# Input stage of a two-layer hybrid attention trunk: token norms from row sums through a diagonal product, norms in quarters, first weights loaded between the blocks of x

## The chip, the cores and the metric

One core of one Trainium2 chip runs the whole program. The metric is the device time in microseconds (us) of one execution; lower is better. Five engines work beside each other and meet only at semaphores: TensorE (PE), VectorE (DVE), ScalarE (ACT), GpSimd (POOL) and SyncE (SP), which here only issues transfers.

## The reference

1040 tokens (16 meta tokens, then 1024 of x) of width 1024 pass two layers. All is float32.

```python
def hybrid_layer(h, pos, norm_g, w_in, w_out, sinks):
    u = rmsnorm(h, norm_g)                       # u = h * rsqrt(mean(h*h) + 1e-6) * g
    proj = jnp.einsum('bld,de->ble', u, w_in)    # 1024 -> 3328
    sb_q, sb_k, sb_v, sb_g, sw_q, sw_k, sw_v, sw_g = jnp.split(proj, splits, axis=-1)
    sb_o = stick_breaking_attention(sb_q, sb_k, sb_v) * jax.nn.silu(sb_g)    # 8 heads of 64
    sw_o = sliding_window_gqa(rope(sw_q), rope(sw_k), sw_v, sinks) * jax.nn.silu(sw_g)
    return h + jnp.einsum('ble,ed->bld', concatenate([sb_o, sw_o]), w_out)

h = concatenate([meta, x])
for l in range(2): h = hybrid_layer(h, ...)
return rmsnorm(h, final_norm_g)[:, 16:]
```

## The kernel before

**Data.** Activations lie transposed: `X[:, k, :]` holds width rows 128k to 128k+127 of all 1040 tokens. Tokens are cut into three chunks, c0 of 400, c1 of 384 and c2 of 256 columns. A projection ("proj j c") is one 128-wide weight tile j times one chunk, for all 8 k. To keep float32 precision each operand is split in a high and a low part (`UH`, `UL` of the normed activations, `WH`, `WL` of the weights), and each k takes three matmuls: UH·WH, UL·WH (L728) and UH·WL (L733); 24 matmuls for a projection. The low part is a subtraction of two tensors in SBUF. The first four tiles of a layer are v, g, q and k of head pair 0 (j = 0, 1, 2, 3).

**Order.** `layer_steps` writes one list of steps, `STEPS`, for both layers. Every engine walks it and does its own part of each step, so the list is each engine's program order. A step that waits holds back all that stands behind it on that engine. Two PSUM banks take turns for the projections: a projection waits until the one two before it has been read. `v` is read by ACT (`vT` copy), `g` by an ACT sigmoid and a DVE product.

**Norm of a chunk.** Squares of X (ACT), sum over k (DVE), a product with `ones` that sums over partitions and gives every partition the row of sums (PE, L676), reciprocal root (ACT, L933), three DVE refinements over the chunk (L1188, L1191, L1194), eight DVE products `mix = X * par * y` (L1198), two ACT copies to `UH` (L939), and the low part `UL`: rows 0 to 3 by POOL (L1491), rows 4 to 7 by DVE (L1205).

**Start.** SP issues ident, meta, the eight blocks of x, then the weights j = 0 and 1. PE transposes each block (L690) into one of two banks; ACT and DVE copy halves to `X` (L948, L1218). In layer 0 the squares are taken over whole chunks of `X` (L959) and summed by a DVE reduction (L1211). When all blocks are in `X`, SP writes `X` to memory (`h_spill`, L627, eight transfers; the residual is read back later) and only then issues the weights j = 2 and on (L621). The split of j = 0 and 1 (`split_w`) comes behind all this: WH by DVE (L1246), WL by POOL (L1504); later weights have both on DVE (L1250). ACT issues the tables `stick`, `cosT`, `sinT` behind the last transposed block.

**Layer end.** The norm of c0 for the next layer is made between the last output projections, c1 and c2 at the next layer's start. After the last layer the same steps run, UH and UL of c0 included, though nobody reads these; then the normed tokens are transposed back and stored.

Of the kernel before, what the change touches and what calls it, by code (L numbers as in the profile page):

```python
# [21 lines left out]
F32 = mybir.dt.float32  # L22
# [13 lines left out]
EPS = 1e-6  # L36
# [55 lines left out]
WL_BY_DVE = range(2, 34)  # L92
# [20 lines left out]
def layer_steps():  # L113
# [5 lines left out]
    def sb_unit(p):  # L119
# [85 lines left out]
    steps = [("split_w", 0), ("split_w", 1)] + flat(sb_unit(0))  # L205
# [31 lines left out]
    for i, c in outs:  # L237
# [16 lines left out]
STEPS = layer_steps()  # L254


def ring_uses():
# [64 lines left out]
 PER_LAYER) = ring_uses()  # L322
LAST_BLOCK = [max(b for b in range(BLOCKS) if q_start(b) < a + width) for a, width in CHUNKS]
# [85 lines left out]
def build(nc, x, meta, params, w_in, w_out, ident_d, rope_d, stick_d, out, h_spill):  # L409
    with ExitStack() as ctx:  # L410
# [57 lines left out]
        wl_made = Tally(sem("wl_made"), TILES, 2)  # L468
        h_ready = Tally(sem("h_ready"), KT * 3, KT * 3)
# [118 lines left out]
        def squared_chunk(c):  # L588

            if c:  # L590
                return mix[:, :, chunk_uses(c)]
            return Vn[:, :, :].rearrange("p a d -> p (a d)")[:, 0:KT * CHUNKS[0][1]].rearrange("p (k n) -> p k n", k=KT)
# [19 lines left out]
        def _(sp):  # L612
            sp.dma_start(ident[:], ident_d).then_inc(ident_in, 16)
            for b in range(BLOCKS):
                sp.dma_start(staged_in(b), x[128 * (b - 1):128 * b, :] if b else meta).then_inc(x_in[b], 16)
            for l in range(DEPTH):
# [12 lines left out]
                for j in range(2):  # L629
                    load(j)  # L630
# [39 lines left out]
        def _(pe):  # L670
# [10 lines left out]
            for b in range(BLOCKS):  # L681
                pe.wait_ge(x_in[b], 16)
                nq = n_queries(b)
                for half in range(2):
                    use = 2 * b + half
                    if use >= 2:
                        pe.wait_ge(in_copied_a if use % 2 == 0 else in_copied_v, use // 2)
                    for i in range(4):
                        t = 4 * half + i
                        ins = pe.transpose(t_bank[use % 2][:, i * nq:(i + 1) * nq],  # L690
                                           staged_in(b)[:, 128 * t:128 * t + 128], ident[0:nq, 0:nq])
                    ins.then_inc(in_turned, 1)
# [4 lines left out]

            for l in range(DEPTH):
                def proj_slot(use):
# [4 lines left out]
                    else:  # L704
# [9 lines left out]
                def project(step):  # L714
# [11 lines left out]
                    for k in range(KT):  # L726
                        for u in (UH, UL):
                            pe.matmul(bank[:, 0:width], WH[:, j % 2, k, :], u[:, k, chunk_uses(c)],  # L728
                                      start=(k == 0 and u is UH), stop=False)
                        if k == 0 and c == 0 and j:  # L730
                            pe.wait_ge(wl_made.sem, wl_made.at(l, j + 1))
                        if c or j:
                            ins = pe.matmul(bank[:, 0:width], WL[:, j % 2, k, :], UH[:, k, chunk_uses(c)],  # L733
                                            start=False, stop=(k == KT - 1))
                    if c == j == 0:

# [809 lines left out]
```

## Time and profile before

| | us |
|---|---|
| median of 3 runs | 1322.46 (1320.25 to 1324.81) |
| the profiled execution, its own time | 1323.66 |
| its span in the trace | 1321.6 |
| PE busy | 1223.2 (93%) |
| PEld busy (weight loads, beside PE) | 1107.6 (84%) |
| DVE busy | 728.3 (55%) |
| ACT busy | 440.3 (33%) |
| POOL busy | 36.2 (3%) |

The span is what the hardware profiler saw from first to last instruction; 2.06 us of the execution's own time lie outside it. PE is busy in almost all of it, so what matters is where it is not, and at which clock it runs.

### The profile page before, as it was taken

How to read it: one execution, taken by the hardware profiler on the slowest of the kernel's cores; microseconds unless marked ns; L12 is line 12 of the kernel's file. 1: busy time of each engine (PE TensorE's matmuls, PEld its weight loads, DVE VectorE, ACT ScalarE, POOL GpSimd, SP SyncE). 2: the span in 40 equal slices, each digit the busy share in tenths (PEclk: the TensorE clock that was granted, in tenths of full speed). 3: DMA queues.
4: the chain of work that ended last, by engine and by line, in shares of the span. 5: the costliest groups of instructions: out<-in, count | busy, mean ns of one | idle time of the engine just before them, and what ended most of it. 6: DMA issues, size and time to landing. Idle time of an engine off the chain costs nothing.

```text
span 1321.6 us, 22286 instructions
## 1 busy us (share of the span) xinstructions
PE 1223.2 (93%) x8824; PEld 1107.6 (84%) x8824; DVE 728.3 (55%) x1376; ACT 440.3 (33%) x1169; POOL 36.2 (3%) x16
## 2 busy tenths in 40 slices
PE   4599999999999998899979999999999999889996
PEld 3598888888888887789969889888888888678995
DVE  5935546556466555734493554555546645573347
ACT  4313324333344342521131332333334333352113
POOL 1200000000000000000040000000000000000001
PEclk7699999999999997899979999999999989789997
DMA  4511101011012111042311101101101211104203
GB/s 163 201 49 32 28 22 33 19 31 33 18 39 62 30 43 39 15 148 65 129 64 49 33 18 32 33 17 33 33 18 39 59 33 39 43 6 157 65 0 127
DMA packets 101685, 69.29 MB, mean 52 GB/s; under 512 B 37824, under 2 KB 95168, under 8 KB 101584
## 3 DMA queue, kind: packets, MB, share of 16 engines
q1 hardware_dynamic: 100720, 66.55, 17.2%
q8 instruction: 71, 1.16, 0.4%
q10 hardware_dynamic: 864, 1.32, 0.3%
q14 instruction: 30, 0.25, 0.1%
HBM read 49.82 MB, written 12.71 MB: 47 GB/s over the span
## 4 chain that ended last, share of the span: by engine, by line
PE 82%; DVE 9%; ACT 4%; issue 3%; DMA 1%; SPq 0%; ACTq 0%; DVEq 0%
PE psum L728 38%; PE psum L733 18%; PE psum L781 7%; PE psum L810 6%; PE psum L793 6%; DVE mix L1198 2%; PE psum L842 2%; PE psum L872 1%; PE psum L879 1%; DMA w_raw<-in_w_out 1%; PE psum L854 1%; DVE dvT L1261 1%; PE psum L690 1%; DVE WH L1246 1%; DVE PT L1194 1%
## 5 line engine op out<-in xcount | busy, mean ns | idle before, releaser
L728 PE MATMUL psum<-UH,WH 128*128 128x384 f32 (+2 forms) x1632 | 551.5, 338 | 22.5 <-DVE WH L1246 10.4
L728 PE MATMUL psum<-UL,WH 128*128 128x384 f32 (+2 forms) x1632 | 535.4, 328 | 0.0
L733 PE MATMUL psum<-UH,WL 128*128 128x256 f32 (+2 forms) x1616 | 526.6, 326 | 0.9 <-DVE WL L1250 0.9
L728 PEld LDWEIGHTS psum<-UH,WH 128*128 128x128 f32 x1632 | 316.4, 194 | 36.8 <-DVE WH L1246 12.5
L728 PEld LDWEIGHTS psum<-UL,WH 128*128 128x128 f32 x1632 | 317.0, 194 | 0.5
L733 PEld LDWEIGHTS psum<-UH,WL 128*128 128x128 f32 x1616 | 312.0, 193 | 1.9 <-DVE WL L1250 1.8
L1093 ACT ACTIVATE PT<-psum 128x512 f32<-128x512 f32 (+5 forms) x260 | 116.7, 491 | 35.0 <-PE psum L793 18.3
L1084 ACT ACTIVATE X<-psum 128x264 f32<-128x264 f32 (+9 forms) x240 | 91.2, 432 | 77.1 <-PE psum L781 76.6
L1330 DVE TENSOR_TENSOR_SCAN X<-X,stick 16x16 f32<-16x16 f32 (+5 forms) x144 | 100.4, 737 | 24.8 <-ACT X L1084 24.4
L793 PE MATMUL psum<-ident,X 128*128 128x128 f32 x576 | 91.2, 283 | 3.7 <-ACT Vn L1047 2.7
L1333 DVE TENSOR_TENSOR_SCAN X<-X 128x352 f32<-128x352 f32 (+4 forms) x96 | 86.3, 939 | 7.5 <-ACT X L1084 7.5
L793 PEld LDWEIGHTS psum<-ident,X 128*128 128x128 f32 x576 | 61.9, 141 | 27.6 <-issue 23.1
L810 PE MATMUL psum<-PT,Vn 128*64 128x128 f32 (+1 forms) x1152 | 84.2, 281 | 0.0
L1250 DVE TENSOR_TENSOR WL<-w_raw,WH 128x1024 fp32r<-128x1024 f32 x64 | 78.4, 1225 | 2.2
L810 PEld LDWEIGHTS psum<-PT,Vn 128*64 128x64 f32 (+1 forms) x1152 | 61.0, 136 | 18.6 <-issue 18.2
L1246 DVE CAST WH<-w_raw 128x1024 fp32r<-128x1024 f32 x68 | 46.5, 686 | 38.4 <-issue 16.4
L975 ACT ACTIVATE mix<-X 128x400 f32<-128x400 f32 (+2 forms) x48 | 23.1, 492 | 133.7 <-DVE X L1269 131.5
L1360 DVE SCALAR_TENSOR_TENSOR mix<-psum,v_end,mix 128x128 f32<-128x128 f32 (+1 forms) x72 | 23.9, 332 | 78.6 <-PE psum L823 78.5
L1269 DVE TENSOR_TENSOR X<-psum,X 128x400 f32<-128x400 f32 (+2 forms) x48 | 24.6, 516 | 76.3 <-PE psum L733 76.3
L842 PE MATMUL psum<-SKH,SQ 64*128 64x144 f32 (+2 forms) x272 | 34.2, 309 | 28.6 <-ACT P_late L1107 15.5
L1491 POOL TENSOR_TENSOR UL<-mix,UH 128x1600 fp32r<-128x1600 f32 (+2 forms) x7 | 25.0, 3576 | 1240.1 <-DVE mix L1198 1228.6
L842 PEld LDWEIGHTS psum<-SKH,SQ 64*128 64x128 f32 (+1 forms) x272 | 26.6, 209 | 36.2 <-issue 29.6
(140 smaller groups left out, 1125.5 us busy)
## 6 DMA issues: line engine op xcount, KB each, us to landing
w_raw<-in_w_in SPq DMA_DIRECT2D x36, 512.0 KB, 3.8
h_spill<-X SPq DMA_DIRECT2D x16, 520.0 KB, 6.1
X<-h_spill SPq DMA_DIRECT2D x16, 520.0 KB, 5.7
w_raw<-in_w_in SPq DMA_DIRECT2D x32, 256.0 KB, 3.7
w_raw<-in_w_out SPq DMA_DIRECT2D x16, 256.0 KB, 3.1
w_raw<-in_w_out SPq DMA_DIRECT2D x32, 128.0 KB, 3.5
out<-X SPq DMA_DIRECT2D x6, 512.0 KB, 3.0
vT<-dvT SPq DMA_DIRECT2D x40, 50.0 KB, 2.0
```

Of the source, the lines that this page charges most:

```text
L728: pe.matmul(bank[:, 0:width], WH[:, j % 2, k, :], u[:, k, chunk_uses(c)], start=(k == 0 and u is UH), stop=False)
L733: ins = pe.matmul(bank[:, 0:width], WL[:, j % 2, k, :], UH[:, k, chunk_uses(c)], start=False, stop=(k == KT - 1))
L781: ins = pe.matmul(z_bank[0:n_queries(b), h, 0:hi - lo], QK[rows, q, queries], QK[rows, k, lo:hi], start=(i == 0), stop=(i == 2))
L793: ins = pe.transpose(bank[:, i * nq:(i + 1) * nq], weights(p, b, h)[:, a:a + 128], ident[:])
L810: ins = pe.matmul(o[64 * h:64 * h + 64, 0:nq], Vn[keys, 9 * (p % 2) + t, 64 * h:64 * h + 64], PT[keys, slots[h] % PT_RING, i * nq:(i + 1) ...
L842: ins = pe.matmul(z, q, keys[rows, first:first + count], start=(i == 0), stop=(i == 2))
L1084: act.activation(weights(p, b, h)[0:n_queries(b), lo:hi], z_bank[0:n_queries(b), h, 0:hi - lo], ACT.Sigmoid, scale=-SCALE).then_inc(z_read ...
L1093: act.activation(PT[0:rows, slot % PT_RING, 0:width], t_bank[use % T_RING][0:rows, 0:width], ACT.Copy)\
L1246: dve.tensor_copy(WH[:, j % 2, :, :], w_raw[:, j % 2, :, :]).then_inc(wh_made.sem, 1)
L1250: dve.tensor_tensor(WL[:, j % 2, :, :], w_raw[:, j % 2, :, :], WH[:, j % 2, :, :].bitcast(F32), ALU.subtract).then_inc(wl_made.sem, 1)
L1330: ins = dve.tensor_tensor_scan(down, down, edge, 1.0, ALU.mult, ALU.max)
L1333: ins = dve.tensor_tensor_scan(down, down, down, P[0:nq, hi:hi + 1], ALU.mult, ALU.bypass)
```

## The change

Layer 0 gets its own list (`LAYER_STEPS[0]`), which begins with the input blocks themselves. In it:

- ACT squares each block of x as it landed, tokens on partitions, and its accumulator gives the sum per token (`in_square`). The root and the three refinements are made on 4 (then 5) numbers a partition. DVE multiplies ident with them, which gives a diagonal matrix (`in_diagonals`), and PE's product of `ones` with it puts the factors in a row on all partitions, in PSUM (`in_rows`). The chunk reductions L1211 and squares L959 are gone.
- The transposed blocks use four banks, not two.
- SP issues w0 behind the second block of x and w1 behind the third. Only w0's low part is left to POOL, in layer 0.
- In both layers the products, UH and UL of a chunk are made in quarters (2 of 8 k), each quarter's UL by DVE; the first projection of a chunk starts when the first quarter is there. POOL does nothing after w0.
- The first projection does its three matmuls for each k like the others.
- Behind the last layer UH and UL of c0 are left out.
- ACT's copy of q, pair 0, now waits for the spill.

```diff
+def norm_pieces(c, ahead):
+    sc, hi, lo = ([(kind, c, part, ahead) for part in range(4)] for kind in ("scale", "high", "low"))
+    return sc[:2] + hi[:1] + lo[:1] + sc[2:3] + hi[1:2] + lo[1:2] + sc[3:] + hi[2:3] + lo[2:3] + hi[3:] + lo[3:]
+IN_GROUPS = [(0, 4), (4, 9)]
+def start_steps(proj_of):
+    T, S, C = ([(kind, b) for b in range(BLOCKS)] for kind in ("in_turn", "in_square", "in_copy"))
+    steps = [S[0], T[0], C[0], S[1], T[1], C[1], S[2], T[2], C[2], ("split_w", 0), S[3], T[3]]
+    steps += [("in_root", 0), ("in_refine", 0), ("in_diag", 0), ("in_row", 0), C[3], T[4], T[5]]
+    spread = {c0[0]: [S[4]], c0[2]: [S[5]], c0[5]: [S[6]], c0[8]: [S[7]], c0[10]: [S[8]]}
...
+    steps += [C[4], C[5], ("in_root", 1), ("in_refine", 1), ("in_diag", 1), ("split_w", 1)] + v[0]
+    steps += [T[6], ("in_row", 1), T[7], C[6]]
+    spread = {c1[1]: [C[7]], c1[6]: g[0] + [T[8]], c1[8]: [C[8], ("in_diag", 2), ("in_row", 2)]}
...
+    steps += v[1] + c2[:4] + g[1] + c2[4:] + v[2] + g[2]
-    steps = [("split_w", 0), ("split_w", 1)] + flat(sb_unit(0))
+    steps = [("split_w", 0), ("split_w", 1)] * (not first) + flat(sb_unit(0))
-            steps += [("norm", 0, 1), ("high", 0, 1)]
+            steps += [("norm", 0, 1)] + norm_pieces(0, 1)[:5]
-            steps.append(("low", 0, 1))
+            steps += norm_pieces(0, 1)[5:]
+IN_BLOCKS = [(0, 4), (4, 7), (7, 9)]
             for b in range(BLOCKS):
                 sp.dma_start(staged_in(b), x[128 * (b - 1):128 * b, :] if b else meta).then_inc(x_in[b], 16)
+                if b in (2, 3):
+                    for to, source in w_parts(0, b - 2):
+                        sp.dma_start(to, source).then_inc(w_landed[b - 2].sem, 16)
...
+            def in_rows(c):
+                pe.wait_ge(in_diag, c + 1)
+                if c == 2:
+                    pe.wait_ge(u_scaled.sem, u_scaled.at(0, KT))
+                for b in range(first, last):
+                    ins = pe.matmul(z_bank[:, c % 2, a:a + nq], ones[0:nq, :], in_diagonal(c)[0:nq, b - first, 0:nq],
+                                    start=True, stop=True)
...
                     for k in range(KT):
+                        if j == 0 and k % 2 == 0:
+                            pe.wait_ge(ul_made.sem, ul_made.at(l, 4 * c + k // 2 + 1))
...
-            def high(l, c, ahead):
+            def high(l, c, part, ahead):
+                if l + ahead == DEPTH:
+                    return
+                act.wait_ge(u_scaled.sem, u_scaled.at(l, KT * (c + 3 * ahead) + 2 * (part + 1)))
...
+            def in_square(b):
+                act.wait_ge(x_in[b], 16)
+                act.activation(Vn[0:nq, spare:spare + 8, :].rearrange("p a d -> p (a d)"), staged_in(b)[:, 0:D], ACT.Square,
+                               accum_out=in_numbers(0)[0:nq, b:b + 1]).then_inc(in_squared, 1)
...
+            def scale(l, c, part, ahead):
+                if l + ahead == 0:
+                    dve.wait_ge(in_row, c + 1)
...
+                    y = z_bank[:, c % 2, 0:CHUNKS[c][1]]
+                for k in range(2 * part, 2 * part + 2):
...
+            def in_diagonals(c):
+                dve.tensor_tensor(in_diagonal(c), ident[:, :].unsqueeze(1).to_broadcast(shape),
+                                  in_numbers(3)[:, first:last].unsqueeze(2).to_broadcast(shape), ALU.mult).then_inc(in_diag, 1)
```

DVE at the program's start. Before, the copies of the blocks into `X` (x of one half block each) up to the first reduction, the norm of c0 and its UL, with the first WH far behind:

```order
L1218 COPY X<-psum 128x4x128 [waits in_turned] x4
L1211 TENSOR_REDUCE dvT<-Vn 128x400 [waits in_squared]
L1218 COPY X<-psum 128x4x128 [waits in_turned]
L1183 TENSOR_SCALAR nsink<-par 128x8 [waits par_in,in_copied_v,in_copied_a]
L1188 SCALAR_TENSOR_TENSOR PT<-psum,PT 128x400 [waits rooted]
L1191 SCALAR_TENSOR_TENSOR PT<-PT 128x400 [waits refined]
L1194 SCALAR_TENSOR_TENSOR PT<-PT 128x400 [waits refined]
L1198 SCALAR_TENSOR_TENSOR mix<-X,par,PT 128x400 [waits refined]
L1198 SCALAR_TENSOR_TENSOR mix<-X,par,PT 128x400 x7
L1218 COPY X<-psum 128x4x128 [waits in_turned]
L1205 TENSOR_TENSOR UL<-mix,UH 128x4x400 [waits u_scaled,uh_made]
```

Now, from behind the copies of blocks 1 and 2 (`small` holds the numbers per token, `PT` the diagonal):

```order
L1330 CAST WH<-w_raw 128x1024 [waits w_landed0]
L1300 TENSOR_SCALAR nsink<-par 128x8 [waits par_in]
L1303 SCALAR_TENSOR_TENSOR small<-small 128x4 [waits in_rooted]
L1306 SCALAR_TENSOR_TENSOR small<-small 128x4 [waits in_refined]
L1309 SCALAR_TENSOR_TENSOR small<-small 128x4 [waits in_refined]
L1316 TENSOR_TENSOR PT<-ident,small 128x512 [waits in_refined]
L1291 COPY X<-psum 128x4x128 [waits in_turned]
L1275 SCALAR_TENSOR_TENSOR mix<-X,par,psum 128x400 [waits in_copied_v,in_copied_a,in_row]
L1275 SCALAR_TENSOR_TENSOR mix<-X,par,psum 128x400
L1275 SCALAR_TENSOR_TENSOR mix<-X,par,psum 128x400 [waits in_row]
L1275 SCALAR_TENSOR_TENSOR mix<-X,par,psum 128x400
L1285 TENSOR_TENSOR UL<-mix,UH 128x2x400 [waits u_scaled,uh_made]
```

The weight's WH stands ahead of the norm of c0, the refinements have become three small instructions and one diagonal, and a UL of two k follows the fourth product.

SP's queue, the program's first transfers, before:

```order
L615 DMA mix<-in_x 128x1024 x3
L615 DMA vT<-in_x 128x1024
L615 DMA kv_stage<-in_x 128x1024 x2
L615 DMA cosT<-in_x 128x1024
L615 DMA sinT<-in_x 128x1024
L621 DMA w_raw<-in_w_in 128x8x128 [waits wl_made] x2
L627 DMA h_spill<-X 128x1040 [waits h_ready] x8
L621 DMA w_raw<-in_w_in 128x8x128 [waits wl_made] x16
```

and now:

```order
L653 DMA mix<-in_x 128x1024 x2
L656 DMA w_raw<-in_w_in 128x8x128
L653 DMA mix<-in_x 128x1024
L656 DMA w_raw<-in_w_in 128x8x128
L653 DMA vT<-in_x 128x1024
L653 DMA kv_stage<-in_x 128x1024 x2
L653 DMA cosT<-in_x 128x1024
L653 DMA sinT<-in_x 128x1024
L672 DMA h_spill<-X 128x1040 [waits in_copied_v,in_copied_a] x8
L662 DMA w_raw<-in_w_in 128x8x128 [waits wl_made] x16
```

The two first weights have moved ahead of five blocks of x. The third weight (j = 2) still stands behind the eight spills.

ACT at the start of layer 1, before, from UH of c1 to the sigmoid of g, c0:

```order
L939 ACTIVATE UH<-mix 128x4x384 [waits u_scaled] x2
L988 ACTIVATE vT<-psum 128x400 [waits proj_full]
L933 ACTIVATE PT<-psum,eps 128x256 [waits refined,norm_full]
L1004 ACT_TABLE_LOAD
L1004 ACTIVATE mix<-psum 128x400 [waits proj_full]
```

and now:

```order
L991 ACTIVATE UH<-mix 128x2x384 [waits u_scaled] x4
L1048 ACTIVATE vT<-psum 128x400 [waits proj_full]
L983 ACTIVATE PT<-psum,eps 128x256 [waits refined,norm_full]
L1064 ACT_TABLE_LOAD
L1064 ACTIVATE mix<-psum 128x400 [waits proj_full]
```

UH comes in four pieces, and the reading of v, c0 still stands behind the last of them.

## Rows read from the trace of the kernel before

**Rows 1.** Timeline, first 80 us: start, length, engine, line, names, count [idle before, releaser]
```profile
15.11 5.53 DVE L1211 TENSOR_REDUCE dvT<-Vn 128x400 f32<-128x3200 f32 x1 [1.63 <-ACT Vn L959]
24.95 4.45 DVE L1198 SCALAR_TENSOR_TENSOR mix<-X,par,PT 128x400 f32<-128x400 f32 x8
...
42.57 8.13 SPq L627 DMA_DIRECT2D h_spill<-X  x8
45.97 1.28 DVE L1246 CAST WH<-w_raw 128x1024 fp32r<-128x1024 f32 x2
...
61.90 0.46 PE L728 MATMUL psum<-UH,WH 128*128 128x384 f32 x1 [3.39 <-DVE UL L1205]
```

**Rows 2.** Chain that ended last, near 78 us: start, length, what
```profile
77.80 0.37 PE psum L728 x2
```

**Rows 3.** Busy time, 45 to 50 us: by engine, then granted clock, DMA share, GB/s
```profile
45.00:50.00 5.00, 3.30 (x10) 3.27 (x11) 4.93 (x6) 0.00 (x0) 3.27 (x2) 0.50 1.02 406
```

**Rows 4.** Timeline: DVE work beside POOL, and the same refinement without it (last row)
```profile
46.73 5.39 POOL L1504 TENSOR_TENSOR WL<-w_raw,WH 128x1024 fp32r<-128x1024 f32 x2 [13.87 <-DVE WH L1246]
47.75 2.15 DVE L1191 SCALAR_TENSOR_TENSOR PT<-PT 128x384 f32<-128x384 f32 x1
...
659.08 0.58 DVE L1191 SCALAR_TENSOR_TENSOR PT<-PT 128x400 f32<-128x400 f32 x1
```

**Rows 5.** Timeline: pieces of the start, on PE
```profile
20.79 1.67 PE L676 MATMUL psum<-dvT,ones 128*128 128x400 f32 x2 [3.21 <-DVE dvT L1211]
...
24.09 0.89 PE L690 MATMUL psum<-ident,cosT 128*128 128x128 f32 x4
```

**Rows 6.** Groups by line and shape: count, then busy us, mean ns of one
```profile
L1434 DVE TENSOR_TENSOR UL<-mix,UH 128x800 fp32r<-128x800 f32 x8 | 7.5, 985 | 0.0
L1218 DVE COPY X<-psum 128x512 f32<-128x512 f32 x8 | 5.5, 686 | 7.2 <-PE psum L690 7.2
L1384 DVE SCALAR_TENSOR_TENSOR small<-small,nsink 128x4 f32<-128x4 f32 x32 | 5.2, 162 | 1.1
L933 ACT ACT_TABLE_LOAD x3 | 3.8, 1283 | 0.1
L939 ACT ACTIVATE UH<-mix 128x1024 fp32r<-128x1024 f32 x4 | 4.2, 1062 | 8.7 <-DVE mix L1198 8.7
```

**Rows 7.** Fifth block of x, first weight: issue; then KB, us to landing
```profile
3.54 0.54 SPq L615 DMA_DIRECT2D kv_stage<-in_x  x1
kv_stage<-in_x SPq DMA_DIRECT2D x1, 512.0 KB, 7.1
...
5.65 5.23 SPq L621 DMA_DIRECT2D w_raw<-in_w_in  x2
w_raw<-in_w_in SPq DMA_DIRECT2D x1, 512.0 KB, 10.7
```

**Rows 8.** The same of the weight j = 2
```profile
50.74 1.53 SPq L621 DMA_DIRECT2D w_raw<-in_w_in  x1
w_raw<-in_w_in SPq DMA_DIRECT2D x1, 512.0 KB, 7.2
```

**Rows 9.** Timeline of the layer boundary
```profile
665.15 4.17 DVE L1261 TENSOR_TENSOR dvT<-dvT,mix 128x384 f32<-128x384 f32 x2
673.49 0.70 PE L728 MATMUL psum<-UH,WH 128*128 128x400 f32 x1 [2.93 <-DVE WH L1246]
679.38 4.33 DVE L1198 SCALAR_TENSOR_TENSOR mix<-X,par,PT 128x384 f32<-128x384 f32 x8
688.68 0.69 PE L728 MATMUL psum<-UH,WH 128*128 128x384 f32 x1 [4.34 <-DVE UL L1205]
699.64 0.49 ACT L1004 ACTIVATE mix<-psum 128x384 f32<-128x384 f32 x1 [3.72 <-PE psum L733]
```

**Rows 10.** Timeline of DVE at the program's end
```profile
1292.87 4.18 DVE L1261 TENSOR_TENSOR dvT<-dvT,mix 128x384 f32<-128x384 f32 x2
1296.96 1.82 DVE L1205 TENSOR_TENSOR UL<-mix,UH 128x1600 fp32r<-128x1600 f32 x1
```

More of the change, by code:

```diff
@@ L91 @@
 PACE = 1.25, 1.25
-WL_BY_DVE = range(2, 34)
 META_UNIT = 8
@@ L586, in chunk_uses, with in_bank, in_numbers, in_diagonal @@
             return slice(CHUNKS[c][0], CHUNKS[c][0] + CHUNKS[c][1])
[L588 to L592, printed above, removed]
+        def in_bank(use):
+            return banks[4 + use % 4]
+        def in_numbers(i):
+            return small[:, i // 2, 9 * (i % 2):9 * (i % 2) + BLOCKS]
+        def in_diagonal(c):
+            first, last = IN_BLOCKS[c]
+            return PT[:, c, 0:128 * (last - first)].rearrange("p (b n) -> p b n", n=128)
         def staged_in(b):
@@ L680, in _, with in_turn @@
             pe.wait_ge(ident_in, 16)
-            for b in range(BLOCKS):
+            def in_turn(b):
                 pe.wait_ge(x_in[b], 16)
@@ L729, in project @@
                                       start=(k == 0 and u is UH), stop=False)
-                        if k == 0 and c == 0 and j:
+                        if k == 0 and c == 0:
                             pe.wait_ge(wl_made.sem, wl_made.at(l, j + 1))
[L732 to L735, printed above, removed]
-                        pe.wait_ge(wl_made.sem, wl_made.at(l, 1))
-                        for k in range(KT):
-                            ins = pe.matmul(bank[:, 0:width], WL[:, 0, k, :], UH[:, k, chunk_uses(0)],
-                                            start=False, stop=(k == KT - 1))
+                        ins = pe.matmul(bank[:, 0:width], WL[:, j % 2, k, :], UH[:, k, chunk_uses(c)],
+                                        start=False, stop=(k == KT - 1))
                     ins.then_inc(proj_full.sem, 1)
@@ L944, in _ @@
-            act.wait_ge(consts_made, 3)
-            for use in range(0, 2 * BLOCKS, 2):
-                b, nq = use // 2, n_queries(use // 2)
-                act.wait_ge(in_turned, use + 1)
+            def high(l, c, part, ahead):
+                if l + ahead == DEPTH:
+                    return
+                act.wait_ge(u_scaled.sem, u_scaled.at(l, KT * (c + 3 * ahead) + 2 * (part + 1)))
+                rows = SPLIT_ROWS[part]
+                act.activation(UH[:, rows, chunk_uses(c)], mix[:, rows, chunk_uses(c)], ACT.Copy).then_inc(uh_made.sem, 1)
@@ L1228, in _, with low @@
[L1228 to L1234 removed]
+            def low(l, c, part, ahead):
+                if l + ahead == DEPTH:
+                    return
+                dve.wait_ge(uh_made.sem, uh_made.at(l, 4 * c + part + 1 + 12 * ahead))
+                dve.wait_ge(u_scaled.sem, u_scaled.at(l, KT * (c + 3 * ahead) + 2 * (part + 1)))
+                rows = SPLIT_ROWS[part]
+                dve.tensor_tensor(UL[:, rows, chunk_uses(c)], mix[:, rows, chunk_uses(c)],
+                                  UH[:, rows, chunk_uses(c)].bitcast(F32), ALU.subtract).then_inc(ul_made.sem, 1)
@@ L1473, in _ @@
                 assert chain.k == DVE_LINKS, f"dve links {chain.k}"
-            norm(DEPTH, 1, 0)
-            norm(DEPTH, 2, 0)
+            for c in (1, 2):
+                norm(DEPTH, c, 0)
+                for part in range(4):
+                    scale(DEPTH, c, part, 0)
             dve.wait_ge(u_scaled.sem, u_scaled.at(DEPTH, 3 * KT))
```

207 lines of the change are left out of this document (113 added, 94 removed).

## The prediction

> **What bounds the kernel now.** I read the busy table first: PE is busy 93% of the span, so only its idle or slow stretches can be won. The timeline shows three, all at norms. First the start. The first projection waits for WH, which DVE makes behind everything else [rows 1]: the reductions of squares (5.53 us for c0), the eight products of c0 (4.45 us), then two casts at 45.97. The spills of X are issued from 42.57. PE starts to project at about 46.6 and runs at granted clock 0.50 of 2.4 GHz, that is 1.2 GHz, from 45 to 50 [rows 3]. After v and g of c0 it stops again and waits 3.39 us for UL of c1, until 61.90 [rows 1]. From there it doesn't stop, and q of c0, the first matmul of weight j = 2, begins at 77.80 [rows 2]. That is the mark that I use: layer 0 from there on is the same code in both kernels.
>
> Second, the layer boundary [rows 9]: PE waits 2.93 us for WH at 673.49 and 4.34 us for UL at 688.68. Third, the end, which DVE bounds [rows 10].
>
> A pattern stands behind the second and third: DVE work of two SBUF inputs stops while POOL works. The refinement of 0.58 us took 2.15 us when it began beside POOL's WL, which held 46.73 to 52.12, and ended about 0.5 us after the first of POOL's two instructions [rows 4]. So POOL's share of UL and WL costs DVE about what it saves.
>
> **The pieces.** A projection is 24 matmuls; two take 0.37 us at full clock on 400 columns [rows 2], so 4.4 us for c0, by columns 4.2 for c1, 2.8 for c2, twice this at 1.2 GHz. A product of 400 columns is 4.45 / 8 = 0.56 us [rows 1], of 384 4.33 / 8 = 0.54 [rows 9], of 256, by columns, about 0.4. A UL quarter of c0 is 0.985 us, a block's copy 0.69, a small instruction on 4 numbers 0.16, UH of 1024 elements 1.06 [rows 6]. UL is also the row that the diagonal and a WL are nearest to: 0.63 us for 512 columns, 1.26 for 1024. No row has a square with an accumulator; below it nothing is cheaper than the 1.06 of the same size, above it I allow 0.3 more.
>
> **When the data land now.** The fifth block of x landed at 3.54 + 7.1 = 10.64, and 512 KB at 406 GB/s [rows 3] are 1.29 us, so the second landed near 6.8, the third 8.05, the fourth 9.35, the eighth 14.5. The first weight landed at 5.65 + 10.7 = 16.35, 1.85 us later [rows 7]. With the weights moved ahead: w0 8.6, third block 9.9, w1 11.75, fourth 13.05, fifth 14.3, eighth 18.2.
>
> **To the row of factors of c0.** DVE has copied the second block at about 10.2, WH of w0 (1.28 / 2) is there at 10.85 [rows 1], and POOL's low part (5.39 / 2 = 2.7) holds until 13.55 [rows 4]. ACT: square of the third block 9.9 to 11.0, table load 1.28 [rows 6], root: 12.5. The refinements have two SBUF inputs, so I let them wait for POOL: 13.55. Three of them with their waits 0.55, the diagonal 0.63, PE's product like the old one 1.67 [rows 5]: the row stands at R = 16.4. Unhindered by POOL it would be 15.35.
>
> The Trainium skill (SBUF — State Buffer, Who interferes with whom) says that a DVE instruction with two SBUF inputs and a GpSimd one that reads SBUF exclude each other for the whole instruction, the later one waiting. That speaks against the one low part left to POOL. By that rule, with which the 2.15 us row agrees, R is 16.4; without it 15.35.
>
> **c0.** DVE has eight products and four UL quarters, 4.45 + 3.94 = 8.4; ACT's squares of blocks 4 to 8 stand between its UH quarters and may hold the last UL a little: R+8.7. PE first transposes blocks 4 and 5 (four halves of 0.89 [rows 5]), then follows the quarters and ends v c0 at about R+10.2.
>
> **c1.** DVE: two copies, refinement, diagonal, WH and WL of w1, copy of block 6: R+13.8. PE meanwhile: block 6, the second row, block 7, until R+15.4, then g c0, 4.4 to 8.8 us by its clock; I take 6, R+21.4. DVE's list has g's product, which waits for that, ahead of the last two products of c1, and behind these the copy of block 8: sigmoid and g product 1.1, products 1.1, copy 0.7: R+24.2 = 40.6. That releases the spill, before at 42.57 [rows 1]. PE goes on with v c1 at about R+25.5, g c1 to R+34, v c2 (held some 2 us by quarters of c2 that stand behind g c1's product on DVE), g c2 to R+41.8 = 58.2.
>
> **The new wait.** SP issues w2 behind the eight spills, and ACT now issues the tables at the same moment, not 5 us ahead. Before, w2 landed at 50.74 + 7.2 = 57.94 [rows 8], 15.4 us after the first spill's issue. The tables are 128 x (456 + 2 x 1040) x 4 bytes = 1.30 MB, 3.2 us at 406 GB/s. So w2 lands between 15.4 (tables fully ahead) and 18.6 us after R+24.2; I take 18.1, as they share the engines: 58.7. WH 0.64 and WL 1.26 behind it: q c0 runs from about 60.2, not 58.2. A restart after a stop costs PE clock: at the boundary v and g of c1 took from 688.68 to 699.64, 10.96 us for 8.4 of work [rows 9], so at most 2.5; I take 1.5 for this shorter stop. 61.7 against 77.80: **16 us**. Bounds: 19.6 where w2 and the clock cost nothing, 12 where g c0 runs wholly at 1.2 GHz and the copies queue up.
>
> **Boundary.** On DVE up to the products of c1, before at 679.38: two sums 4.18 us beside POOL [rows 9], about 1.1 without, −3.1; UL of c0 whole on DVE, 3.94 for 1.82, +2.1; two WL, +2.5; refinements at 0.58 instead of beside POOL, −3.6; part of the gain is lost waiting for PE's last projections: net −1.5. The last product pair of c1 ends at 677.9 + 4.33 + 1.9 = 684.1. What is late next is a bank: v c1 needs v c0 read by ACT, whose copy stands behind the fourth UH quarter: 684.1 + 0.75 + 0.5 = 685.4, against 688.68, 3.3 earlier. The stop is 1.4 us, not 4.34, so up to 2.2 of the restart comes back. I take **5 us** between 3.3 and 7 (the bank costs nothing).
>
> **End.** DVE loses the stall of the sums (3.1) and the UL of 1.82 [rows 10], but PE's last two projections start only 1.1 earlier, two products being moved behind the add that frees their bank: **1.7 us**, bounds 1.1 and 3.
>
> **Costs at nothing.** Squares of blocks 4 to 8 hide beside DVE's products; UH quarters have a fixed cost more per piece, hidden likewise. q's new wait for the spill: the spill is through before q c0 is projected; if not, it is part of the new wait.
>
> **Sum.** 16 + 5 + 1.7 = 22.7 us, from 1323.66 to 1301.0. The median of the runs is 1.2 below that execution, so 1299.8, say 1300.
>
> **Rivals.**
> - *w2 is no bound and the clock comes early* (12%). For it: spills of 8.13 us of issue [rows 1] may overlap tables that went first. 19.6 + 3 (g c0 at full clock, R a us less), 7 and 1.7: 31 us, 1291.5.
> - *The weights hold SP's issue* (12%). The two weights took 5.23 us to issue against 0.54 for a block [rows 7]. If w1 holds SP again, blocks 4 to 8 land up to 4.7 us later. Against it: the engines have work meanwhile, and fewer transfers are pending. The start gives 11, the boundary 3.3: 16 us, 1306.5.
> - *It doesn't do what it says* (3%): the projections begin early but w2 is not there until about 77, so that all is given back. That needs the spill to start at 59 instead of 40.6. 1320.
> - *Slower* (3%): PE's work in pieces never brings the clock up, and the whole first stage of layer 0 (v, g of c1 and c2, q and k: 36.8 us at full clock) runs at 1.2 GHz. Price 36.8, so 1337; it decides from 22.7 us of work at half rate, three fifths of it. Against it: before, too, work without stops followed 61.90, and q ran at full rate at 77.80 [rows 2].
>
> The Trainium skill (DMA: Bandwidth & Descriptors, Issuing engines are not separate DMA queues) says that transfers of ACT and SP interleave on the same 16 engines. By that rule w2 comes at the late end; no row before has both at once, so it only leans to the forecast.
>
> **Numbers.** The forecast has 70%, its own range 1294 to 1306 (the bounds of the three terms taken together). The range to the neighbours on both sides is 1292 to 1308. A measurement of this kernel can tell about 0.3% (4 us) from no change: faster 94%, within 3%, slower 3%.
>
> **What would show it.** In the new trace: the row product ends near 16.4; first projection matmul near 19 to 20; spills' issue near 40.6; q's first matmul near 60 with w2's WH just ahead of it; v c1 of layer 1 about 3 us earlier relative to layer 1's first WH wait, right behind ACT's vT copy; no DVE instruction of 4 us behind the last projections. Wrong would make it: a refinement that doesn't wait for POOL, late blocks, a granted clock of 0.5 far past 30 us, or WH of j = 0 in layer 1 later than before.

## The result, and the profile after

| | before | after |
|---|---|---|
| median of the runs, us | 1322.47 (4 runs) | 1291.97 (4 runs, 1288.35 to 1294.01) |
| profiled execution: time, span | 1323.66, 1321.6 | 1294.01, 1292.2 |
| PE busy, DVE busy, POOL busy | 1223.2, 728.3, 36.2 | 1215.8, 703.9, 2.6 |

The ratio of after to before is 0.9766, 95% interval 0.9735 to 0.9798: 30.5 us faster, where 22.5 were forecast. The time lies 0.03 us below the low end of the range.

The page's busy table of after shows that DVE lost 24 us and PE only 7, so most of the gain is PE time that was idle:

```profile
PE 1215.8 (94%) x8836; PEld 1103.3 (85%) x8836; DVE 703.9 (54%) x1393; ACT 438.9 (34%) x1193; POOL 2.6 (0%) x5
```

The timeline of after, first 60 us (start, length, engine, line, names, count, [idle before, releaser]), answers to [rows 1, 4, 5]:

```profile
10.53 2.35 POOL L1582 TENSOR_TENSOR WL<-w_raw,WH 128x1024 fp32r<-128x1024 f32 x1 [10.09 <-DVE WH L1330]
12.59 0.31 DVE L1303 SCALAR_TENSOR_TENSOR small<-small 128x4 f32<-128x4 f32 x1 [2.06 <-ACT small L1011]
14.08 2.19 PE L749 MATMUL psum<-PT,ones 16*128 16x16 f32 x8 [2.29 <-DVE PT L1316]
16.30 2.26 DVE L1275 SCALAR_TENSOR_TENSOR mix<-X,par,psum 128x400 f32<-128x400 f32 x4 [1.68 <-PE psum L749]
19.61 0.67 PE L781 MATMUL psum<-UH,WH 128*128 128x400 f32 x1
27.22 0.94 PE L749 MATMUL psum<-PT,ones 128*128 128x128 f32 x6
28.79 0.43 PE L781 MATMUL psum<-UH,WH 128*128 128x400 f32 x1
33.26 1.04 PE L737 MATMUL psum<-ident,sinT 128*128 128x128 f32 x8
34.90 0.45 ACTq L1023 DMA_DIRECT2D cosT<-in_rope  x1
37.58 3.17 SPq L672 DMA_DIRECT2D h_spill<-X  x4
37.87 1.22 PE L749 MATMUL psum<-PT,ones 128*128 128x128 f32 x4 [3.57 <-DVE PT L1316]
39.21 0.52 PE L781 MATMUL psum<-UL,WH 128*128 128x384 f32 x1
45.68 12.02 SPq L662 DMA_DIRECT2D w_raw<-in_w_in  x3
51.12 0.39 PE L781 MATMUL psum<-UH,WH 128*128 128x256 f32 x1 [1.85 <-DVE UL L1285]
52.04 0.42 PE L785 MATMUL psum<-UH,WL 128*128 128x256 f32 x1
55.36 0.69 DVE L1330 CAST WH<-w_raw 128x1024 fp32r<-128x1024 f32 x1 [2.12 <-PE psum L785]
```

and its chain of waits, where q of c0 starts (the mark of [rows 2]):

```profile
58.10 0.36 PE psum L781 x2
```

The row of factors is there at 16.30, the first projection starts at 19.61. From 19.61 PE stops only twice for over a microsecond, 3.57 us at 37.87 and 1.85 at 51.12, both behind DVE. Behind each it runs slow for a while: matmuls of 384 columns take 0.52 us until 41 us, and of 256 columns 0.42 until 55 us, where 0.34 and 0.28 are its full rate. w2, issued at 45.68, lands 8.7 us later, at 54.4; its WH at 55.36 waited for PE to be done with v of c2, not for the landing. q of c0 starts at 58.10 against 77.80: **19.7 us**.

The layer boundary of after, which answers to [rows 9]:

```profile
645.29 1.23 DVE L1345 TENSOR_TENSOR dvT<-dvT,mix 128x384 f32<-128x384 f32 x2
653.17 0.45 PE L781 MATMUL psum<-UH,WH 128*128 128x400 f32 x1 [2.47 <-DVE WH L1330]
657.93 2.21 DVE L1275 SCALAR_TENSOR_TENSOR mix<-X,par,PT 128x384 f32<-128x384 f32 x4
664.78 0.48 ACT L1048 ACTIVATE vT<-psum 128x400 f32<-128x400 f32 x1
665.32 0.45 PE L781 MATMUL psum<-UH,WH 128*128 128x384 f32 x1 [1.80 <-ACT vT L1048]
675.61 0.49 ACT L1064 ACTIVATE mix<-psum 128x384 f32<-128x384 f32 x1 [2.07 <-PE psum L785]
```

g of c1 is read at 675.61 instead of 699.64 [rows 9], 24.03 earlier; 19.67 of it had been gained by the boundary's first add (655.42 before, 635.75 after). The boundary gives **4.4 us** between these two executions. The size depends on PE's clock: in all runs with the order of after (after, experiments 2, 3, 4, 6, 7 and 10) v of c1 starts 29.55 to 29.58 us behind that add, but g of c1 is read 39.8 to 39.9 us behind it in five of them, and 38.3 in experiments 3 and 4, where PE stopped 4.02 us for WH and not 2.5. With those two the boundary would give 5.9. The end, which answers to [rows 10]:

```profile
1260.62 0.58 DVE L1256 SCALAR_TENSOR_TENSOR PT<-psum,PT 128x400 f32<-128x400 f32 x1 [2.42 <-ACT PT L983]
...
1266.21 1.24 DVE L1345 TENSOR_TENSOR dvT<-dvT,mix 128x384 f32<-128x384 f32 x2
...
1266.35 0.39 PE L781 MATMUL psum<-UH,WH 128*128 128x256 f32 x1 [1.11 <-DVE X L1353]
1271.05 0.55 DVE L1256 SCALAR_TENSOR_TENSOR PT<-psum,PT 128x384 f32<-128x384 f32 x1
```

From the first refinement of c0 to that of c1 it is 1271.05 − 1260.62 = 10.43 us; before 1300.47 − 1286.19 = 14.28. The end gives **3.85 us**. The three terms make 27.9 of the 29.4 us between the spans. The other 1.5 lie in the middle of layer 1, where both kernels have the same code. From the WH cast at 729.80 to the one at 748.57 it took before's profiled execution 18.77 us, with granted clock 0.83 in 728 to 738; after took 17.18 for the same work (705.77 to 722.95), with 1.00 in 704 to 714. Such differences come without any change: from the copy of v's last columns (L1305 before, L1389 after) to the first refinement at the end, the twelve profiled executions of this document take 577.1 to 583.6 us for the same code; before takes 581.8, and experiment 5, which is before up to there, 577.1. So the 1.5 us are taken as chance, not as the change.

### The profile page after: what moved, and what is told of

The parts are those of the page before. It is cut to its first block, busy times and chain, and to the rows that moved or that the text cites. A ratio compares the mean times of both kernels' runs of the same rounds, so it can differ in the third digit from the quotient of the medians.

```text
span 1292.2 us, 22354 instructions
## 1 busy us (share of the span) xinstructions
PE 1215.8 (94%) x8836; PEld 1103.3 (85%) x8836; DVE 703.9 (54%) x1393; ACT 438.9 (34%) x1193; POOL 2.6 (0%) x5
## 4 chain that ended last, share of the span: by engine, by line
PE 84%; DVE 7%; ACT 3%; issue 3%; DMA 2%; SPq 1%; ACTq 0%; DVEq 0%
PE psum L781 39%; PE psum L785 19%; PE psum L827 7%; PE psum L856 6%; PE psum L839 6%; DVE mix L1275 2%; PE psum L888 2%; PE psum L918 1%; PE psum L925 1%; PE psum L900 1%; DMA w_raw<-in_w_out 1%; PE psum L869 1%; DVE WL L1334 1%; ACT P_late L1167 1%; PE psum L798 1%
## 5 line engine op out<-in xcount | busy, mean ns | idle before, releaser
L785 PE MATMUL psum<-UH,WL 128*128 128x384 f32 (+2 forms) x1632 | 532.4, 326 | 1.5 <-DVE WL L1334 1.5
L785 PEld LDWEIGHTS psum<-UH,WL 128*128 128x128 f32 x1632 | 315.3, 193 | 2.8 <-DVE WL L1334 2.7
L1334 DVE TENSOR_TENSOR WL<-w_raw,WH 128x1024 fp32r<-128x1024 f32 x67 | 82.1, 1225 | 2.3
L856 PEld LDWEIGHTS psum<-PT,Vn 128*64 128x64 f32 (+1 forms) x1152 | 61.0, 136 | 18.6 <-issue 18.2
L827 PE MATMUL psum<-qk_even 64*128 64x264 f32 (+9 forms) x360 | 46.3, 342 | 3.7 <-DVE qk_even L1367 2.0
```

What stands on the lines that cost most here:

```text
L827: ins = pe.matmul(z_bank[0:n_queries(b), h, 0:hi - lo], QK[rows, q, queries], QK[rows, k, lo:hi], start=(i == 0), stop=(i == 2))
L856: ins = pe.matmul(o[64 * h:64 * h + 64, 0:nq], Vn[keys, 9 * (p % 2) + t, 64 * h:64 * h + 64], PT[keys, slots[h] % PT_RING, i * nq:(i + 1) ...
L1334: dve.tensor_tensor(WL[:, j % 2, :, :], w_raw[:, j % 2, :, :], WH[:, j % 2, :, :].bitcast(F32), ALU.subtract).then_inc(wl_made.sem, 1)
```

## Experiments

All ten kernels were timed beside the kernel before; "q" below is the start of q of c0 in layer 0, as first matmul in the timeline (57.94 in after).

**1. Quarters.** PE waits for all of UL before the first projection of each chunk:

```diff
-                        if j == 0 and k % 2 == 0:
-                            pe.wait_ge(ul_made.sem, ul_made.at(l, 4 * c + k // 2 + 1))
+                        if j == 0 and k == 0:
+                            pe.wait_ge(ul_made.sem, ul_made.at(l, 4 * c + 4))
```

> The changed kernel, but PE's first projection of a chunk waits for all four UL quarters, not quarter by quarter. Theory (quarters feed PE while DVE still works, and keep it at full clock): v c0 of layer 0 starts at 24.8 us instead of 19.6, after 5 us of idle, so partly at 1.2 GHz, ends near 31 instead of 26.2; block 6, the second row and c1 follow 3.5 to 5 us later; q c0 near 63 to 66 instead of 58.1; time 5 to 9 us over 1292. Rival (DVE is the bound of the start anyway, PE's early start only makes it wait later): q c0 at 58 to 60, time within 2 us of 1292.

Measured: 1303.78 us, ratio 0.9837 [0.9821, 0.9852]. Its timeline:

```profile
25.30 0.67 PE L781 MATMUL psum<-UH,WH 128*128 128x400 f32 x1 [5.27 <-DVE UL L1285]
...
27.44 0.54 PE L781 MATMUL psum<-UH,WH 128*128 128x400 f32 x1
...
59.36 0.55 PE L781 MATMUL psum<-UH,WH 128*128 128x256 f32 x1 [4.81 <-DVE UL L1285]
```

The first projection starts 5.7 us later and q 9.8 us later (67.74). Half of the start's gain is the quarters, and about 4 us of that is not the wait itself: behind the stop of 5.27 us a matmul of 400 columns takes 0.54 us and not 0.35, until 31 us, and the stop before c2 has grown from 1.85 to 4.81. At the boundary the quarters bring little. From its first add to the copy of v's last columns (L1389) it takes 43.67 us here and 44.59 in after, but PE stopped 4.00 us for WH here, as in experiments 3 and 4, and against their 43.0 the quarters bring 0.7: v of c1 starts 30.25 us behind the add, not 29.55.

**2. Weights behind x.** SP issues w0 and w1 behind the last block; WH of w0 is cast behind the copy of block 3.

> The changed kernel with both first weights issued behind the last block of x again, and WH of the first made by DVE just ahead of the products of c0 instead of ahead of the refinements. Theory (the sums per token are what brings the start forward; a weight is not needed until the products): w0 lands near 16.4, WH holds the products from 16.3 to about 17.1, POOL's low part holds the first UL a little; first projection matmul at 20.5 to 21 instead of 19.6; q c0 near 59 to 60; time 1 to 2 us over 1292. Rival (the early weights carry the start): all 7.8 us by which w0 lands later show, q c0 at 64 or more.

Measured: 1294.07 us, 0.9766 [0.9746, 0.9787], the same as after. WH waits 2.69 us for w0 and is made at 16.20. But no weight stands ahead of the third block of x, so its square starts at 8.84 and not 9.80 and the refinements at 11.63 and not 12.59; with POOL still idle the first takes 0.16 us and not 0.31. The row product starts at 12.97 instead of 14.08. The first projection comes at 20.34, q at 58.77, 0.8 us later. Where the weights' transfers stand among the blocks hardly matters. That the split of w0 must not stand behind the norm of c0, as it did before, no run tests by itself.

**3. w2 ahead of the spill.** SP issues the weight j = 2 at 13.36, before it waits to spill:

```diff
+                else:
+                    load(2)
...
                 for j in range(2, IN_TILES + 2):
-                    load(j)
+                    if l or j > 2:
+                        load(j)
```

> The changed kernel with the third weight (j = 2) issued by SP ahead of the eight spills. Theory (PE came to q c0 only when w2 was there already: its WH began when PE left v c2, not when the transfer landed): no change, q c0 at 58.1 plus or minus 0.5, time within 1 us of 1292. Rival (w2's landing behind the spills is the new wait, as predicted): q c0 2 to 3 us earlier.

Measured: 1293.25 us, 0.9767 [0.9751, 0.9783]: no gain. WH of w2 stands at 56.77 behind 2.27 us of waiting for PE, as in after. q starts at 59.62, 1.7 us later than in after, mostly because PE's slow matmuls behind its stop of 3.58 us last until 43.5 us here and until 41.1 in after. In after w2 is not what q waits for.

**4. The add at the end behind all products** (the order of before for the last two products of c0):

```diff
-            steps += [("norm", 0, 1)] + norm_pieces(0, 1)[:5]
+            steps += [("norm", 0, 1)] + norm_pieces(0, 1)[:5 if first else 8]
```

> The changed kernel, but at the end of layer 1 the add of c1 that frees PE's bank stands behind all eight products of c0 again, not six; layer 0 untouched. From the first refinement of c0 to the first of c1 at the end the old kernel took 14.28 us, the changed one 10.43. Theory (PE's stop of 2.2 us lets its clock fall, one of 1.1 us does not): PE stops 2.2 us ahead of the last two projections, these take 5.3 us instead of 3.1, the mark is 13.3 to 14. Rival (only the order of DVE's work counts): the projections take 3.1 us, the mark is 11.5.

**5. Before, with UH and UL of c0 left out behind the last layer**, and nothing else changed (nobody reads them, so no output depends on it).

> The kernel before, with the high and low products of the first chunk skipped at the end of layer 1 (there they feed nothing that follows except as part of the last normalization's chunk 0, so this run leaves that part out), and all else as before. It asks what the end's gain of 3.8 us in the changed kernel is made of. Theory (the clock): in the kernel before, TensorE's stop of 2.2 us is followed by two projections that take 5.3 us at half clock, where the changed kernel takes 3.1 us after a stop of 1.1 us; with the products skipped and the one long sum of 4.2 us still there, the stop and the slow restart stay, so the end gains only the product's own place, about 0.9 us (ratio 0.9993). Rival (VectorE's work alone): the stall of the sums beside ScalarE's products and the product on VectorE are what was paid, so skipping them gives 3 us or more (ratio 0.9975 or less), and the sum takes about 1.2 us.

Measured: experiment 4 gives 1292.04 us, 0.9745 [0.9712, 0.9779], which alone says nothing about 1 us; experiment 5 gives 1321.41, 0.9979 [0.9965, 0.9994], 0.21% or 2.8 us faster than before (0.8 to 4.6 by the interval). Timeline of experiment 5 at the end:

```profile
1282.69 0.57 DVE L1190 SCALAR_TENSOR_TENSOR PT<-psum,PT 128x400 f32<-128x400 f32 x1 [2.42 <-ACT PT L933]
...
1289.35 1.24 DVE L1265 TENSOR_TENSOR dvT<-dvT,mix 128x384 f32<-128x384 f32 x2
1289.49 0.39 PE L728 MATMUL psum<-UH,WH 128*128 128x256 f32 x1 [2.20 <-DVE X L1273]
1290.08 0.28 PE L728 MATMUL psum<-UL,WH 128*128 128x256 f32 x1
...
1293.99 0.56 DVE L1190 SCALAR_TENSOR_TENSOR PT<-psum,PT 128x384 f32<-128x384 f32 x1
```

and of before, what stood beside its sums of 4.18 us [rows 10]:

```profile
1291.94 4.02 POOL L1491 TENSOR_TENSOR UL<-mix,UH 128x1600 fp32r<-128x1600 f32 x1 [596.50 <-DVE mix L1198]
1295.44 0.41 PE L728 MATMUL psum<-UL,WH 128*128 128x256 f32 x1
```

The mark falls from 14.28 to 11.30 us, though PE still stops 2.20 us there. The theory of the clock (13.4 in experiment 5, 13.3 to 14 in experiment 4) is wrong, and the rival is right: UH and UL were what was paid. POOL's UL ended at 1295.96, and the two sums of SBUF inputs, started at 1292.87, ended at 1297.05 behind it; then DVE's own UL of 1.82 us came. The run leaves out both and doesn't separate them. In experiment 4 the mark is 11.47: 1.0 us over after's, with the stop back at 2.20 us. So the end's 3.85 us are 2.8 for UH and UL left out and 1.0 for the add that stands earlier.

The clock was not the same in these runs. Behind the stop of 2.20 us the last projection (24 matmuls of 256 columns) ran at full rate to its end in experiments 4 and 5, in 2.9 us, and in before at half rate from 1294.4 on, in 4.1. In before that cost nothing, since DVE was held by the sums and the UL until 1298.78. Had experiment 5 met the same clock, its mark would be longer by up to 1.2 us, an estimate from 4.1 − 2.9, and the share of UH and UL smaller by as much.

**6. The two stops closed, and 7. the same with w2 ahead of the spill:**

```diff
-    steps += [T[6], ("in_row", 1), T[7], C[6]]
-    spread = {c1[1]: [C[7]], c1[6]: g[0] + [T[8]], c1[8]: [C[8], ("in_diag", 2), ("in_row", 2)]}
+    steps += [T[6], ("in_row", 1), T[7], C[6], ("in_diag", 2)]
+    spread = {c1[1]: [C[7]], c1[6]: g[0] + [T[8]], c1[9]: [C[8], ("in_row", 2)]}
...
-    steps += v[1] + c2[:4] + g[1] + c2[4:] + v[2] + g[2]
+    steps += c2[:4] + v[1] + c2[4:] + g[1] + v[2] + g[2]
```

> The changed kernel with two orders of the start altered: the diagonal of chunk 2 made right behind the copy of block 6 and its row product three places later, and the first four pieces of chunk 2 made ahead of v of chunk 1, the rest ahead of g of chunk 1. This should close TensorE's two stops of 3.6 and 1.9 us behind VectorE. Theory: the weights of j=2, issued behind the first spill, then become the bound (they land near 55 us and nothing hides them any longer), so q of chunk 0 starts near 56 us and not 58.1, and about 2 us come off (ratio to before 0.975). Rival: the weights land earlier as well or don't matter, all of the two stops and their slow restarts comes off, q starts near 51 us, 6 to 8 us off.

> The run before this one with the weights of j=2 issued by SP ahead of the first spill as well. Theory: nothing but TensorE's own work is left between v of chunk 0 and q of chunk 0: q starts near 50 us, about 8 us before the changed kernel's (time near 1284 against 1292). Rival: the spill's 1.8 MB ends later behind the weights or the weights' buffer is not what was late, and the time stays within 2 us of the run without this edit.

Measured: experiment 6 gives 1294.45 us, 0.9775 [0.9755, 0.9795], and experiment 7 1284.22 us (1283.72 to 1286.76), 0.9703 [0.9682, 0.9723]. Timeline of experiment 6:

```profile
54.84 0.69 DVE L1330 CAST WH<-w_raw 128x1024 fp32r<-128x1024 f32 x1 [8.28 <-DMA w_raw<-in_w_in]
55.59 0.45 PE L781 MATMUL psum<-UH,WH 128*128 128x400 f32 x1 [4.50 <-DVE WH L1330]
56.85 0.70 PE L785 MATMUL psum<-UH,WL 128*128 128x400 f32 x1 [0.63 <-DVE WL L1334]
57.35 0.54 PE L781 MATMUL psum<-UH,WH 128*128 128x400 f32 x1
```

and of experiment 7:

```profile
47.83 0.69 DVE L1333 CAST WH<-w_raw 128x1024 fp32r<-128x1024 f32 x1 [1.78 <-PE psum L788]
50.42 0.35 PE L784 MATMUL psum<-UH,WH 128*128 128x400 f32 x1
```

Two bounds lie side by side. With the stops closed, w2 binds: PE waits 4.50 us for it, q starts 2.35 us earlier (55.59), and the slow matmuls of 0.54 us behind the stop take more than that back: the projection ends at 63.77, in after at 62.31. With w2 early as well, q starts at 50.42, 7.5 us earlier, and the time falls by 7.75 (by the ratios to before, 0.9703 against 0.9766, 8.3). Either edit alone brings nothing. (The spill is eight transfers of 520 KB, 4.2 MB, not the 1.8 of the expectation.)

**8. Also v of c0 placed between the pieces of c1 in layer 1**, so that ACT reads its bank sooner:

```diff
-            start = [("norm", 1, 0)] + norm_pieces(1, 0) + v[0] + [("norm", 2, 0)] + g[0] + norm_pieces(2, 0)
+            c1 = norm_pieces(1, 0)
+            start = [("norm", 1, 0)] + c1[:8] + v[0] + c1[8:] + [("norm", 2, 0)] + g[0] + norm_pieces(2, 0)
```

> The run before this one with v of chunk 0 placed behind the first eight of chunk 1's eleven pieces at the start of layer 1, so that ScalarE reads v of chunk 0 out of its bank earlier. Theory: TensorE's stop of 1.8 us at the layer boundary, which is a bank not yet read by ScalarE, and the half clock behind it go: about 3 us more than the run without it (near 1281). Rival: the pieces then come later for v of chunk 1, and the stop only changes its releaser (VectorE in place of ScalarE): within 1 us of the run without it.

Measured: 1284.24 us (1281.96 to 1288.55), 0.97 [0.9679, 0.9722]. PE's stop at the bank is gone from its trace, and the boundary (from the add of c1's columns between the products of c0, at 638.12 us, to L1389's copy) takes 33.45 us against 35.53 in experiment 7, 2.1 less. Most of that isn't the edit: experiments 3 and 4, without it, take 33.9 and 34.0 where PE stopped 4.02 us for WH as here (4.00) and not 2.51 as in experiment 7. Against them the edit brings 0.5 us, and the time, the same as experiment 7's, agrees. The profiled execution was the slowest of the five, 1288.55, as its middle of layer 1 took 583.6 us, the longest of all, and experiment 7's 578.4, with the same code.

**9. WL of j = 0 and 1 in layer 1 by POOL again.**

> The changed kernel with one part undone: the low parts WL of the weights j=0 and j=1 of layer 1 are made by POOL again and not by VectorE. Theory (two-input VectorE work stands still while POOL works): VectorE saves 2.45 us of its own, but the refinements of chunk 1 and with them its products come 1 us or more later than in the changed kernel, and the time is the same or 1 to 2 us longer (1292 to 1294). Rival (POOL works beside VectorE): the products of chunk 1 come 2.4 us earlier; PE then still waits for its bank, so the time falls by at most 1.8 us, and no refinement takes over 0.6 us.

Measured: 1293.69 us, 0.9774 [0.9746, 0.9802]. Its timeline:

```profile
652.45 5.38 POOL L1587 TENSOR_TENSOR WL<-w_raw,WH 128x1024 fp32r<-128x1024 f32 x2 [639.55 <-DVE WH L1330]
652.88 0.55 DVE L1256 SCALAR_TENSOR_TENSOR PT<-psum,PT 128x384 f32<-128x384 f32 x1
653.47 2.12 DVE L1259 SCALAR_TENSOR_TENSOR PT<-PT 128x384 f32<-128x384 f32 x1
655.62 2.62 DVE L1262 SCALAR_TENSOR_TENSOR PT<-PT 128x384 f32<-128x384 f32 x1
658.27 2.21 DVE L1275 SCALAR_TENSOR_TENSOR mix<-X,par,PT 128x384 f32<-128x384 f32 x4
```

The refinement that reads PSUM and one SBUF tensor takes its 0.55 us beside POOL; the two that read two SBUF tensors each end about 0.5 us after one of POOL's two instructions. The products start 23.27 us after the boundary's first add (635.00), against 22.18 in after: 1.1 later, as the theory said. POOL's help costs DVE more than it saves. The Trainium skill (SBUF — State Buffer, Who interferes with whom) has this as a rule, one SBUF input free and two excluded; these rows agree with both halves. PE also waits 2.17 us for POOL's WL of j = 0 at 655.22, where it waited 0.62 for DVE's in after. The times (1293.69 and 1291.97) are too near each other to price all this.

**10. All squares ahead of the root of c0:**

```diff
-    steps += [("in_root", 0), ("in_refine", 0), ("in_diag", 0), ("in_row", 0), C[3], T[4], T[5]]
+    steps += S[4:] + [("in_root", 0), ("in_refine", 0), ("in_diag", 0), ("in_row", 0), C[3], T[4], T[5]]
```

(and the squares no longer between the pieces of c0).

> The changed kernel with one part undone: ScalarE makes the squares of all nine blocks before the root of chunk 0, instead of the four that chunk 0 needs. The last block lands near 18 us, so the row of factors of chunk 0 should stand near 21.5 to 22 and not at 16.3, 5.5 us later. Theory (the row of factors is on the path one for one): q of chunk 0 starts 5 to 6 us later than in the changed kernel, about 63.5 us, time near 1297.5. Rival (later work has slack and absorbs it, as TensorE's two stops of 3.6 and 1.9 us shrink and no squares are left to hold ScalarE): q starts at most 2 us later, time under 1294.5. A third outcome, more than 8 us later, would mean that the longer stop ahead of the row brings TensorE's clock down and that this counts too.

Measured: 1300.68 us, 0.9833 [0.9803, 0.9863]. The row stands at 24.60, 8.3 us later and not 5.5, because ACT runs five squares at 1.28 us each behind one another. q starts at 64.13, 6.2 us later than in after, and so is all of layer 0 behind it; the profiled executions differ by 6.1 us, the medians by 8.7. The path itself is one for one, or nearly: PE's stop behind the diagonal of c2 ends at 45.72 and not at 37.87, 7.85 us later. The next one ends at 57.40 and not at 51.12, 6.3 later, as the granted clock behind the first was 1.00 from 45 to 55 us here, and 0.79 and 0.87 from 35 to 45 in after. So the rival falls, the theory had the mechanism, and I had the row's delay too small. The third outcome, over 8 us in the start, didn't come: PE stopped 11.15 us ahead of the row product, but was slow only in it and the transposes behind it, and ran the projections from 27.90 on at full rate.

## Why the prediction was too slow

**Right.** (R is when the row of factors stands, 16.4 in the forecast and 16.30 in the trace.) The first projection at 19.61 (19 to 20), c0's last UL at R+8.5 (8.7), v c0 read at R+10.0 (10.2), the products of c1 at R+13.5 (13.8); v of c1 in layer 1 behind ACT's vT copy (it ends at 665.26, PE starts at 665.32) with a stop of 1.80 us (1.4 said); sums at 1.23 us (1.1); the boundary, 4.4 us for 5, within the 4.4 to 5.9 that the same code gave. The sum's shape, start first and two small terms, held.

**Right by luck: R.** POOL's WL ended at 12.88 and not at 13.55, and the refinements began at 12.59, so POOL held them by 0.15 us and not by the 1.05 between 15.35 and 16.4. In return three refinements with their waits, the diagonal and the row product took 0.74, 0.69 and 2.19 us for 0.55, 0.63 and 1.67. The misses cancel.

**The step that failed: "The new wait".** PE's own work was to end at R+41.8 = 58.2; on top of it the prediction put 3.5 us, w2 landing at 58.7 with WH behind it (q at 60.2) and 1.5 for a restart. None of it came. w2 lay at 54.4 in SBUF, 4.3 us early, when v of c2 still held its WH slot; WH was made from 55.36 on under PE's work on g of c2, and q followed at 57.94 without a stop. Of the 4.3 us, 1.3 are the transfer, 16.8 us behind the spill's issue and not 18.1: ACT issued the tables at 34.5 to 35.4, 3 us ahead of the spill, and not with it. The other 3.0 are the spill, issued at 37.58 and not 40.6. Experiment 3 shows that w2 was no bound: issued 32 us earlier, no gain. Yet experiment 6 shows how near it was: with PE's own two stops closed q came only 2.35 us earlier. The rule of the Trainium skill that I cited with this step (DMA: Bandwidth & Descriptors, Issuing engines are not separate DMA queues) leaned to the late end; 16.8 lies in the middle of 15.4 and 18.6, and no run separated the two queues.

**The step behind it: block 6, the second row and block 7 "until R+15.4, then g c0 ... I take 6, R+21.4".** PE did the first three in 2.7 us and not 5.2, at full rate, with the row product of c1 in 0.94 us and not 1.67; g of c0 then ran from 28.79 (R+12.5) to 33.26, 4.5 us for 6. It ended 4.3 us earlier than said, and through DVE's list the spill came 3.0 us earlier. The pieces had been priced by rows of the old start, where PE worked behind long stops: 1.67 is of a product behind 3.21 us [rows 5], 0.50 of v of c0 [rows 3]. But g of c0 itself ran at full rate there too, from about 54 us on:

```profile
50.00:55.00 5.00, 5.00 (x24) 4.93 (x23) 4.96 (x6) 0.19 (x1) 2.12 (x1) 0.81 1.01 347
55.00:60.00 5.00, 3.51 (x20) 3.18 (x18) 3.44 (x5) 4.36 (x5) 3.62 (x1) 1.00 0.64 181
```

(before, busy time by engine, then granted clock, DMA share and GB/s, as in [rows 3]). The next step missed the other way. PE stopped 3.57 us for DVE's diagonal of c2, which stands behind two products and the copy of block 8, stopped 1.85 us again, and ran slow behind both. So PE's own work ended at 57.94, where 58.2 was said: that the 4.3 us were given back so exactly is luck.

Together these make the start 19.7 and not 16. I had its bound at 19.6 "where w2 and the clock cost nothing". The first did happen; the clock did cost, behind the two stops. The first rival, 12%, said that w2 is no bound, and that came; its 31 us are near the 29.4 between the spans partly by chance, as it had 22.6, 7 and 1.7 for the terms that measured 19.7, 4.4 and 3.85.

**The size that was off: the end, 3.85 for 1.7.** I counted PE's earlier start (1.1, and experiment 4 against after gives 1.0) and left out that DVE comes to c1's refinements directly from the stalled sums and the UL. Experiments 4 and 5 put 2.8 us on these (not the whole 3.1 + 1.8, since DVE then waits for PE's last projection, 1.69 us in experiment 5). The two terms add, and my bounds of 1.1 and 3 held them apart.

**What was no error.** 1.5 us are the low clock in layer 1 of before's profiled execution, which no reading of the code could give.

**A slip in the range.** The bounds of the three terms make 16.4 and 29.6 us together. From the median before, 1322.46, that is 1292.9 to 1306.1; the low end of 1294 was counted from the profiled execution, 1323.66.

Sum of the differences from the forecast: start +3.7, boundary −0.6, end +2.1, chance 1.5. That is 6.7 of the 7.8 us between my 22.7 and the 30.5 of the medians; the rest is that the medians lie differently far from their profiled executions (2.0 us after, 1.2 before).

## What to carry to other kernels

When a change lets PE start early and keeps it busy, don't price its work by the rate that it had behind stops in the old trace (experiment 1 puts about 4 us of 10 on that): work out which stops are gone and which are new, and price a slow stretch behind the new ones. Before calling a transfer "the new wait", list what holds its buffer and PE at that time: two bounds that end within a few us of each other can make each single repair worthless and both together worth 8 us (experiments 3, 6 and 7). A second engine's help can cost more than it saves where the first one's instructions read two SBUF tensors meanwhile (experiment 9). And before a few us are put down to an edit, look how much the same code differs between executions.

The best version is that of experiment 7, with experiment 8 no worse: 1284.2 us, 7.8 below after.

## What the runs showed of the hardware

(Granted clock 1.00 is 2.4 GHz, 0.50 is 1.2.)

- The granted clock of a window and the length of matmuls don't always agree. In experiment 1 the clock column reads 1.00 from 26 to 30 us, while matmuls of 400 columns take 0.54 us; from 32 us, also at 1.00, they take 0.34. In after, eight transposes at 9.82 took 1.97 us at "1.00", in experiment 3 at 10.28 1.10. The length of a matmul was the safer sign here.
- What a stop costs depends on what stands behind it. Behind 5.27 us (experiment 1) the slow stretch fell on projections, behind 11.15 us (experiment 10) on a row product and transposes. And equal stops differ: behind 3.57 us the granted clock was 0.79 in 35 to 40 us and 0.87 in 40 to 45 (after), behind 3.58 us 0.67 and 0.64 (experiment 3), behind 3.59 us 1.00 (experiment 10); behind 2.20 us at the end the last projection took 4.1 us (before) and 2.9 (experiments 4 and 5). What decides was not isolated.
- One issue in the SP queue took 2.58 us (the fourth block of x in after, 4.17 to 6.75) where its neighbours took 0.45 to 0.58. In before such a stall fell on the weights (5.23 us for two, [rows 7]), in experiment 2 as well (5.11 us). It cost nothing in after, where no engine waits for a transfer of x behind 9.82 us.
